# Running sums of the log decays: formed once in the projections and loaded per chunk, instead of formed per chunk by TensorE

## The chip, the cores and the metric

One core of a Trainium2 chip. The engines are TensorE (PE; its weight loads are listed apart as PEld), VectorE (DVE), ScalarE (ACT), GpSimd (POOL) and SyncE (SP), which issues all the DMAs of this kernel. The metric is the device time of one execution in microseconds; the kernel before takes 2838.83 us, the median of three runs (2835.25 to 2843.82).

## The reference

A trunk layer with three token mixers, sequence 2048, width 1024, all float32. The change touches only the third mixer, the gated delta rule (8 value heads, 4 query/key heads of 128), where each head has a scalar log decay per token:

```python
g = jnp.cumsum(log_a, axis=-1)
diff = g[..., :, None] - g[..., None, :]
decay_strict = masked_exp(diff, strict)
decay_causal = masked_exp(diff, causal)
m = jnp.einsum('bhntk,bhnsk->bhnts', k, kb) * decay_strict
sol = lax.linalg.triangular_solve(eye + m, rhs, ...)
a_qk = jnp.einsum('bhntk,bhnsk->bhnts', q, kb) * decay_causal
q_inter = q * jnp.exp(g)[..., None]
k_state = kb * jnp.exp(g_last[..., None] - g)[..., None]
```

So per chunk and head the kernel needs a 128x128 matrix exp(g_t - g_s) for t >= s, the vectors exp(g_t) and exp(g_last - g_s), and exp(g_last).

## The kernel before

Four stages follow one another with barriers between: `norm_and_transpose` (to 84 us), `project` (to 1638), `recur` (to 2287) and `merge`.

`project` forms all projections as 80 pairs of column tiles `p`, with a Strassen-like scheme; ACT rounds each weight block (`high_part`), POOL forms the rest (`low_part`), PE multiplies. At its end POOL fills masks (`fill_masks`), among them `causal`. The log decays of all 16 chunks and 8 heads already lie in SBUF as `ab[:, :, 0:V]`, a token per partition.

`recur` walks 16 chunks (windows) `w` of 128 tokens. The order on each engine is written out by hand, and while window `w` is computed, the preparation of `v = w+1` is woven in. For the decays, POOL multiplies the causal mask by the log decays in two fp32r parts (`log_decays`, L1454, result `la_t`); PE sums them with a mask of later tokens (`decays_between`, L1554 with `later_r`) and with ones (`decays_from_start`, L1554 with `ones_r`), four instructions of 512 columns each; ACT takes the exponentials from PSUM into `dec` and `eg` (L1833, L1839); POOL multiplies `dec` by minus beta (`weighted_decays`, L1464), and DVE makes `ak` and `aq` with it (`an_keys` L2019, `an_queries` L2024).

The inverse of the triangular matrix runs through DRAM. SP writes `ak` out (L1383), waits, and loads its 16x16 diagonal blocks as `X` (L1386). DVE sets their diagonal (`unit_diagonal`, L2028) and substitutes in 14 steps (L2040, L2043), interleaved with its other work; ACT copies the results as `XI` and `XT` (L1904, L1905); SP writes them (L1395, L1397), and loads whole matrices `T` and `R` (L1400, L1403) for window `v`. PE then doubles the block size three times (`level_w`, `level_z`: L1657, L1677 and others). On SP's queue a window is thus: T, R, `zin` (1 MB) and `hin` (1.25 MB) for the window after, the keys (512 KB, `load_k`, landing in `w_raw`), two stores `yh` and `yc` (256 and 512 KB), `ak` out (512 KB), X, and then XI and XT again. `load_k` waits for `keys` of DVE, the stores for the results, `ak` out for DVE's `an_keys`.

Two more waits matter. PE's `products_ds(w, 0)` (the second L1714 of a window) waits for XT of `v`. DVE's first instruction of a window, `pair_kq` (L2058), waits for `hx_inv`, which ACT makes (L1847) after `key_norms`, which waits for PE's `norms` (L1550).

Of the kernel before, what the change touches and what calls it, by code (L numbers as in the profile page):

```python
# [22 lines left out]
P = 128  # L23
# [481 lines left out]
def project(nc, dm, io, keep, front, h_dram, s_dram, y_dram, g_dram):  # L505
# [78 lines left out]
    with ExitStack() as c:  # L584
# [13 lines left out]
        X, Y, Z = ([bank(f"p_{n}{i}") for i in range(2)] for n in "xyz")  # L598
        own_sems = []
# [16 lines left out]
        zeroed, step, masks_set, masks_cut = sem("zeroed"), sem("step"), sem("masks_set"), sem("masks_cut")  # L616

# [14 lines left out]
        t2 = craw[:, 0, :, 3:3 + 2 * BLK]  # L632
        form_place = {P1: wide(work[:]), P5: wide(work[:]), P2: wide(lows_of(P5)), P6: t2, P4: wide(ring[:]), P3: wide(lows_of(P3))}
# [42 lines left out]
        with nc.Block() as block:  # L676
            @block.sync
            def _(sp):
# [37 lines left out]
                for p in range(N):  # L716
                    q = before(p)
# [35 lines left out]
                sp.wait_ge(keys_in, 16)  # L753
                for r in range(RING):
# [4 lines left out]
            def _(pool):  # L759
# [16 lines left out]
                for p in range(N):  # L776
                    for of, j in ((p + 1, P1), (p, P4), (p + 1, P2), (p, P3), (p + 1, P6), (p + 1, P5), (p + 1, P7)):
# [6 lines left out]
                fill_masks(pool, {**keep["masks"], **front["masks"]}, masks_set, masks_cut)  # L784

            @block.tensor
            def _(pe):
# [22 lines left out]

                for p in range(N):
                    q = before(p)
# [22 lines left out]
            def _(act):  # L835
# [108 lines left out]
                for p in range(N):  # L944
                    q, more = before(p), p + 1 < N
# [61 lines left out]
            def _(dve):  # L1007
# [8 lines left out]
                def token_sum(sb, j):  # L1016
# [7 lines left out]
                    elif of == P7:  # L1024
                        if k.start == 0:
                            dve.wait_ge(b_in["b22"], 16 * sb)
                        else:
# [193 lines left out]
                for p in range(N):  # L1221
                    q, more = before(p), p + 1 < N
# [52 lines left out]
def recur(nc, dm, io, keep, front, lead, s_dram, y_dram):  # L1275
# [18 lines left out]
    with ExitStack() as c:  # L1294
# [3 lines left out]
        col, neg_b = sb("col", [P, 3, win, V]), sb("neg_b", [P, win, V])  # L1298
        la_parts = sb("la_parts", [P, 2, win, V], F32R)
        la_t = sb("la_t", [P, 2, V, P], F32R)  # L1300
        ones_r, later_r = sb("ones_r", [P, P], F32R), sb("later_r", [P, P], F32R)
# [25 lines left out]
        count(m_ssq=2, m_ga=2, m_gb=2, m_kq=2, m_vt=2, m_ks=2, m_kt=1, m_hvt=1, m_w=2 * levels, m_z=2 * levels,  # L1327
              m_hs=7, m_e=2, m_o=2, m_ds=2, m_hkt=1, m_ho=1, m_hds=1, m_hn=1, m_n=2)
        count(rn_ready=4, dec_ready=2, eg_ready=2, vt_ready=2, kt_ready=1, hv_ready=1, w_ready=2 * levels,
# [1283 lines left out]
```

## Time and profile before

| | |
|---|---|
| median of 3 runs | 2838.83 us (2835.25 to 2843.82) |
| span of the profiled execution, first to last instruction | 2836.0 us |
| own time of that execution beyond its span | not listed; the median is 2.8 us above the span |
| PE busy, PEld busy | 2729.1 us (96%), 2284.9 us (81%) |
| DVE, ACT, POOL busy | 1843.0, 1240.6, 1471.9 us |
| DMA | 366.05 MB, 45.0% of 16 engines |

The page gives averages over four stages, and the change acts on one of them, so the stage `recur` is read by itself: its engines' busy time by window, the timeline of one window, and the order of SP's issues. A number in brackets behind a timeline row is how long the engine stood idle before it, and what released it. TensorE's clock is 1.00 of full in the steady windows; it is at half in part of window 0.

### The profile page before, as it was taken

How to read it: one execution, taken by the hardware profiler on the slowest of the kernel's cores; microseconds unless marked ns; L12 is line 12 of the kernel's file. 1: busy time of each engine (PE TensorE's matmuls, PEld its weight loads, DVE VectorE, ACT ScalarE, POOL GpSimd, SP SyncE). 2: the span in 40 equal slices, each digit the busy share in tenths (PEclk: the TensorE clock that was granted, in tenths of full speed). 3: DMA queues.
4: the chain of work that ended last, by engine and by line, in shares of the span. 5: the costliest groups of instructions: out<-in, count | busy, mean ns of one | idle time of the engine just before them, and what ended most of it. 6: DMA issues, size and time to landing. Idle time of an engine off the chain costs nothing. (4 is left out here: it accounts for less than half of the span.)

```text
span 2836.0 us, 39388 instructions
## 1 busy us (share of the span) xinstructions
PE 2729.1 (96%) x14135; PEld 2284.9 (81%) x14135; DVE 1843.0 (65%) x2902; ACT 1240.6 (44%) x2154; POOL 1471.9 (52%) x1135
## 2 busy tenths in 40 slices
PE   6899999999998999999999979999999989999999
PEld 5788888888886888888888868888888867888887
DVE  6677777773338788888732258888888855445453
ACT  6443444444444434343444335565556533222221
POOL 0545555454445455555544556667776534453541
PEclk9999999999999999999999979999999989999999
DMA  5333333333453333333334356555556557455552
GB/s 173 99 110 97 112 91 103 108 107 91 119 158 115 122 97 106 88 112 108 97 101 119 97 145 154 146 134 132 134 152 155 135 173 239 157 183 169 177 174 76
DMA packets 536937, 366.05 MB, mean 129 GB/s; under 512 B 65462, under 2 KB 469032, under 8 KB 536744
## 3 DMA queue, kind: packets, MB, share of 16 engines
q1 hardware_dynamic: 536744, 363.52, 45.0%
q8 instruction: 115, 1.88, 0.3%
q14 instruction: 78, 0.64, 0.1%
HBM read 251.27 MB, written 112.20 MB: 128 GB/s over the span
## 5 line engine op out<-in xcount | busy, mean ns | idle before, releaser
L767 POOL TENSOR_TENSOR w_low<-w_raw,w_high 128x512 fp32r<-128x512 f32 x480 | 686.1, 1435 | 635.7 <-ACT w_high L845 635.7
L799 PE MATMUL p_x<-h_high,w_high 128*128 128x512 f32 x1280 | 501.1, 391 | 16.8 <-POOL w_low L767 7.5
L799 PE MATMUL p_x<-h_low,w_high 128*128 128x512 f32 x1280 | 500.5, 391 | 0.0
L799 PE MATMUL p_x<-h_high,w_low 128*128 128x512 f32 x1280 | 500.5, 391 | 0.0
L845 ACT ACTIVATE w_high<-w_raw 128x512 fp32r<-128x512 f32 x480 | 297.1, 626 | 246.3 <-PE p_z L799 139.9
L799 PEld LDWEIGHTS p_x<-h_high,w_high 128*128 128x128 f32 x1280 | 241.7, 189 | 69.3 <-POOL w_low L767 7.6
L799 PEld LDWEIGHTS p_x<-h_low,w_high 128*128 128x128 f32 x1280 | 241.7, 189 | 50.5
L799 PEld LDWEIGHTS p_x<-h_high,w_low 128*128 128x128 f32 x1280 | 241.7, 189 | 50.2
L799 PE MATMUL p_z<-h_high,w_low 128*128 128x512 f32 x640 | 249.0, 389 | 0.0
L799 PE MATMUL p_z<-h_high,w_high 128*128 128x512 f32 x640 | 249.0, 389 | 0.0
L799 PE MATMUL p_z<-h_low,w_high 128*128 128x512 f32 x640 | 249.0, 389 | 0.0
L2407 PE MATMUL b_o<-m_yh,m_wo_high 128*128 128x512 f32 x512 | 201.2, 393 | 19.1 <-DVE m_yl_lead L2543 12.5
L1090 DVE TENSOR_TENSOR c_raw<-p_z,u 128x512 f32<-128x512 f32 x72 | 49.8, 691 | 245.2 <-PE p_x L799 188.9
L2368 POOL TENSOR_TENSOR m_wo_low<-m_wo_raw_lead,m_wo_high 128x512 fp32r<-128x512 f32 x86 | 117.8, 1372 | 172.6 <-ACT m_wo_high L2462 172.6
L2407 PE MATMUL b_o<-m_yh,m_wo_low 128*128 128x512 f32 x512 | 200.4, 391 | 0.0
L767 POOL TENSOR_TENSOR w_low<-w_s,w_high 128x512 fp32r<-128x512 f32 x80 | 114.9, 1436 | 98.0 <-ACT w_high L845 97.3
L1106 DVE SCALAR_TENSOR_TENSOR ring<-c_raw,cols,ring 128x512 f32<-128x512 f32 x128 | 142.3, 1112 | 4.6
L1475 POOL TENSOR_TENSOR dx<-hin 128x256 f32<-128x256 f32 x112 | 76.6, 684 | 130.7 <-ACT hx L1858 117.5
L2506 DVE TENSOR_TENSOR w_raw<-b_o,ring 128x512 f32<-128x512 f32 x96 | 65.9, 691 | 118.2 <-PE b_o L2407 97.0
L799 PEld LDWEIGHTS p_z<-h_high,w_high 128*128 128x128 f32 x640 | 120.1, 188 | 25.1 <-DVE c_raw L1090 0.2
L799 PEld LDWEIGHTS p_z<-h_low,w_high 128*128 128x128 f32 x640 | 120.1, 188 | 24.9
L799 PEld LDWEIGHTS p_z<-h_high,w_low 128*128 128x128 f32 x640 | 120.1, 188 | 24.9
(299 smaller groups left out, 6082.2 us busy)
## 6 DMA issues: line engine op xcount, KB each, us to landing
w_raw<-in_w_in_dram SPq DMA_DIRECT2D x160, 512.0 KB, 5.2
branch_scratch<-ring SPq DMA_DIRECT2D x176, 256.0 KB, 5.2
gate_scratch<-ring SPq DMA_DIRECT2D x96, 256.0 KB, 6.0
ring<-gate_scratch SPq DMA_DIRECT2D x96, 256.0 KB, 4.0
hin<-branch_scratch SPq DMA_DIRECT2D x16, 1280.0 KB, 11.4
zin<-branch_scratch SPq DMA_DIRECT2D x16, 1024.0 KB, 7.0
m_wo_raw_lead<-in_w_out_c_dram SPq DMA_DIRECT2D x43, 256.0 KB, 3.0
xin<-in_x_dram SPq DMA_DIRECT2D x16, 512.0 KB, 4.0
```

The lines of the kernel that those rows point to most:

```text
L767: nc.gpsimd.tensor_tensor(wl[:, j, :, :], place(p, j), wh[:, j, :, :].bitcast(F32), ALU.subtract).then_inc(low, 1)
L799: x = nc.tensor.matmul(to[:], w[:, j, k, :], h[:, j, k, :], start=(opens and k == 0 and a == 0), stop=(k == HK - 1 and a == 2), skip_group ...
L845: fn(wh[:, j, :, :], place(p, j), ACT.Copy).then_inc(high, 1)
L1090: tt(of_unit(p, 1, 1), Z[p % 2][:], u3[:], ALU.add).then_inc(c22, 1)
L1106: link(stt(out, src, w, out, ALU.mult, ALU.add))
L1475: tt(free_ap(dx[:, l % 2, :], 0, halves), left, mid, ALU.subtract)
L2368: tt(wl[:, u % SLOTS, :, :], wraw(u), raw(wh[:, u % SLOTS, :, :]), ALU.subtract).then_inc(w_low, 1)
L2407: x = nc.tensor.matmul(bank, w[:, u % SLOTS, k, :], y(4 * i + k), start=(i < 3 and k == 0 and a == 0), stop=(i != 2 and k == 3 and a == 2))
L2506: tt(to, bank, gt[:, b, :], ALU.mult).then_inc(gated, 1)
```

## The change

In `project`, PE forms once four sums over all chunks (causal, after, all, and `centred`, the sum counted from the middle of the chunk) into PSUM before pair 8; ACT copies them at pair 9; PE transposes two of them before pair 10, ACT copies at 11, and SP writes both to DRAM at pair 12. `causal` is filled by POOL before pair 3, two masks by DVE at pair 6. In `recur`, SP loads per chunk two rows of 1024 sums spread over all 128 partitions (512 KB each, 4 KB per partition): `rows_centred` and `rows_start`. POOL subtracts the column sums and takes the minimum with 0 (`exponents`); ACT takes the exponentials from SBUF. The eight matrix instructions of L1554 of each chunk, `log_decays`, and `columns` are gone, and the waits on PSUM banks that they needed.

```diff
@@ project, PE
+                    for i, which in enumerate((causal[:], after, keep["ones"][:], centred)):
+                        x = nc.tensor.matmul(sums_bank[:, i, :], which, ab[:, :, 0:dm.vh], start=True, stop=True)
+                    for i, at in enumerate((0, 3)):
+                        x = nc.tensor.transpose(rows_bank[:, i, :], kept_sums[:, at, :], keep["ident"][:])
@@ recur, SP
+                def load_centred(v):
+                    wait(sp, v - 1, "diff_ready", 1)
+                    sp.dma_start(rows_centred[:].rearrange("p h n -> p (h n)"), bass.AP(rows.tensor, (win + v) * V * P, [[0, P], [1, V * P]])
+                                 ).then_inc(centred_in, 16)
+                def load_start(v):
+                    wait(sp, v - 1, "eg_ready", 1)
+                    sp.dma_start(rows_start[:].rearrange("p h n -> p (h n)"), bass.AP(rows.tensor, v * V * P, [[0, P], [1, V * P]])
+                                 ).then_inc(start_in, 16)
...
+                sp.dma_start(col[:].rearrange("p i w c -> p (i w c)"), front["decay_sums"]).then_inc(col_in, 16)
+                load_centred(0)
+                load_start(0)
                 load(0)
...
                         blocks_out(w + 1)
+                        if w + 2 < win:
+                            load_start(w + 2)
                         inverses_back(w + 1)
+                        if w + 3 < win:
+                            load_centred(w + 3)
@@ recur, POOL
-                def log_decays(v):
-                    wait(pool, v - 1, "m_ga", 2)
-                    for i in range(2):
-                        tt(la_t[:, i, :, :], free_ap(masks["causal"][:], 0, [[0, V], [1, P]]), spread(la_parts[:, i, v, :].bitcast(F32), P),
-                           ALU.mult).then_inc(sems["la_ready"], 1)
+                def exponents(v):
+                    pool.wait_ge(centred_in, 16 * v + 16)
+                    wait(pool, v - 1, "aq_ready", 2)
+                    tt(dec[:], rows_centred[:], spread(col[:, 3, v, :], P), ALU.subtract).then_inc(sems["diff_ready"], 1)
+                    wait(pool, v, "diff_ready", 1)
+                    nc.gpsimd.tensor_scalar(dec[:], dec[:], 0.0, None, ALU.min).then_inc(sems["diff_ready"], 1)
@@ recur, PE (main loop)
-                    if 0 < w < win - 1:
-                        decays_between(v)
                     level_z(w, 4)
...
-                    if 0 < w < win - 1:
-                        decays_from_start(v)
                     level_w(w, 5)
@@ recur, ACT
+                    wait(act, v, "diff_ready", 2)
                     for g in range(2):
-                        wait(act, v, "m_gb", g + 1)
-                        fn(four(dec, g), M[g][:], ACT.Exp).then_inc(sems["dec_ready"], 1)
+                        fn(four(dec, g), four(dec, g), ACT.Exp).then_inc(sems["dec_ready"], 1)
...
-                    for g in range(2):
-                        wait(act, v, "m_ga", g + 1)
-                        fn(four(eg, g), M[2 + g][:], ACT.Exp).then_inc(sems["eg_ready"], 1)
+                    act.wait_ge(start_in, 16 * v + 16)
+                    fn(eg[:], rows_start[:], ACT.Exp).then_inc(sems["eg_ready"], 1)
```

PE's row in a steady window, before (b_m are PSUM banks, `la_t` the masked log decays):

```order
6879 L1657 MATMUL b_g<-T,ak 128x64 x8
6880 L1604 MATMUL b_m<-ident,qkn 128x128 x4
6881 L1610 MATMUL b_m<-ident,hin 128x128 x4
6882 L1554 MATMUL b_m<-la_t,later_r 128x512 x4
6883 L1677 MATMUL b_g<-W,R 128x64 x8
6884 L1577 MATMUL b_m<-qkn 128x256 x4
6885 L1628 MATMUL b_h<-kql 128x128 x4
6886 L1554 MATMUL b_m<-la_t,ones_r 128x512 x4
6887 L1657 MATMUL b_g<-T,ak 128x64 x8
```

and the same place after:

```order
6875 L1697 MATMUL b_g<-T,ak 128x64 x8
6876 L1644 MATMUL b_m<-ident,qkn 128x128 x4
6877 L1650 MATMUL b_m<-ident,hin 128x128 x4
6878 L1717 MATMUL b_g<-W,R 128x64 x8
6879 L1619 MATMUL b_m<-qkn 128x256 x4
6880 L1668 MATMUL b_h<-kql 128x128 x4
6881 L1697 MATMUL b_g<-T,ak 128x64 x8
```

Eight instructions between the first and the second `level_w` are gone, and nothing else moved.

SP's queue in a steady window, after (`w_raw` is where the keys land):

```order
200 L1453 DMA T<-inverse_scratch 128x8x128
201 L1456 DMA R<-inverse_scratch 128x8x128
202 L1407 DMA rows_centred<-decay_rows_scratch 128x1024
203 L1424 DMA zin<-branch_scratch 128x16x128
204 L1425 DMA hin<-branch_scratch 128x20x128
205 L1418 DMA w_raw<-branch_scratch 128x8x128
206 L1430 DMA y_scratch<-yh 128x4x128
207 L1432 DMA y_scratch<-ring 128x8x128
208 L1436 DMA an_scratch<-ak 128x8x128
209 L1439 DMA X<-an_scratch 64x16x16
210 L1412 DMA rows_start<-decay_rows_scratch 128x1024
211 L1448 DMA inverse_scratch<-XI 64x16x16
```

The row is that of before, with `rows_centred` put in ahead of `zin` and `rows_start` put in behind X.

SP's queue at the start of `recur`, after; before, the five rows of `col`, `rows_centred` and `rows_start` are not there:

```order
176 L1468 DMA col<-decay_sums_scratch 128x512
177 L1407 DMA rows_centred<-decay_rows_scratch 128x1024
178 L1412 DMA rows_start<-decay_rows_scratch 128x1024
179 L1424 DMA zin<-branch_scratch 128x16x128
180 L1425 DMA hin<-branch_scratch 128x20x128
181 L1474 DMA inverse_scratch<-S 128x8x128 x2
182 L1418 DMA w_raw<-branch_scratch 128x8x128
183 L1407 DMA rows_centred<-decay_rows_scratch 128x1024
184 L1412 DMA rows_start<-decay_rows_scratch 128x1024
185 L1436 DMA an_scratch<-ak 128x8x128
186 L1439 DMA X<-an_scratch 64x16x16
```

All five added loads of the start stand ahead of the first `ak` out and the first X.

## Rows read from the trace of the kernel before

**Rows 1.** Busy us by stretch: PE, PEld, DVE, ACT, POOL, clock, DMA share, GB/s.
```profile
1757.76:1795.45 37.69, 37.06 (x296) 32.89 (x295) 31.88 (x91) 22.56 (x44) 26.70 (x24) 1.00 0.58 146
1720.07:2212.85 492.78, 483.11 (x3824) 427.99 (x3823) 414.74 (x1170) 292.98 (x560) 347.17 (x312) 1.00 0.58 145
```
**Rows 2.** Timeline of PE, one window: start us, duration us, line, output and inputs.
```profile
1761.11 1.22 PE L1554 MATMUL b_m<-la_t,later_r 128*128 128x512 f32 x4
1762.17 1.89 PE L1677 MATMUL b_g<-W,R 128*128 128x64 f32 x16
...
1765.68 1.05 PE L1628 MATMUL b_h<-kql 128*128 128x128 f32 x8
1766.49 1.17 PE L1554 MATMUL b_m<-la_t,ones_r 128*128 128x512 f32 x4
1767.49 1.90 PE L1657 MATMUL b_g<-T,ak 128*128 128x64 f32 x16
...
1785.80 1.06 PE L1714 MATMUL b_m<-e,ks 128*128 128x128 f32 x8
...
1791.09 1.88 PE L1550 MATMUL b_m<-w_raw,ones 128*128 128x512 f32 x4
```
**Rows 3.** Timeline of DVE, the same window: its ends and its waits.
```profile
1757.76 0.69 DVE L2058 TENSOR_TENSOR kql<-hin,hx_inv 128x512 f32<-128x512 f32 x1 [2.30 <-ACT hx_inv L1847]
...
1774.55 0.07 DVE L2028 MEMSET X<- 64x16 f32 x1
...
1782.76 0.42 DVE L2079 COPY A<-b_h 64x256 f32<-64x256 f32 x1 [0.21 <-PE b_h L1630]
...
1795.45 0.69 DVE L2058 TENSOR_TENSOR kql<-hin,hx_inv 128x512 f32<-128x512 f32 x1 [2.24 <-ACT hx_inv L1847]
```
**Rows 4.** Timeline of ACT, end of the same window.
```profile
1784.82 0.38 ACT L1904 ACTIVATE XI<-b_m 64x256 f32<-64x256 f32 x1 [2.15 <-DVE b_m L2043]
1785.10 0.36 ACT L1905 ACTIVATE XT<-b_m 64x256 f32<-64x256 f32 x1
```
**Rows 5.** Timeline of SP's DMA issues: start us, us of issuing.
```profile
1750.79 0.37 SPq L1400 DMA_DIRECT2D T<-inverse_scratch  x1
...
1762.77 0.36 SPq L1365 DMA_DIRECT2D w_raw<-branch_scratch  x1
...
1766.89 0.36 SPq L1383 DMA_DIRECT2D an_scratch<-ak  x1
1770.77 0.60 SPq L1386 DMA_DIRECT2D X<-an_scratch  x1
...
1788.46 0.37 SPq L1400 DMA_DIRECT2D T<-inverse_scratch  x1
```
**Rows 6.** DMA issues in 1740 to 2200 us: KB each, median us to landing.
```profile
X<-an_scratch SPq DMA_DIRECT2D x12, 64.0 KB, 2.7
```
**Rows 7.** Waits in 1740 to 2200 us: us in total, times, longest.
```profile
DVE X L2028 <- DMA X<-an_scratch: 2.2, 4, 0.9
```
**Rows 8.** DMA in 1750 to 1776 us, 40 slices of 0.65 us.
```profile
DMA  3004899999999999999998699999997100550000
GB/s 49 0 9 97 243 345 329 292 289 291 289 291 291 289 294 299 291 290 290 290 290 214 169 291 354 333 345 349 344 346 235 39 0 0 50 51 0 0 0 0
```
**Rows 9.** Timeline of POOL, the same window.
```profile
1763.17 2.37 POOL L1464 TENSOR_TENSOR dec<-dec,db 128x1024 f32<-128x1024 f32 x1 [3.11 <-ACT dec L1833]
1765.49 1.90 POOL L1489 TENSOR_TENSOR ks<-kt,col 128x1024 f32<-128x1024 f32 x1
...
1770.32 3.75 POOL L1454 TENSOR_TENSOR la_t<-causal,la_parts 128x1024 fp32r<-128x1024 f32 x2
```
**Rows 10.** Start of `recur`: DMA in 1640 to 1656 us, 40 slices of 0.4 us.
```profile
GB/s 159 128 236 324 337 348 346 302 287 274 283 297 298 298 293 287 289 289 291 294 310 344 348 346 344 348 348 346 346 348 347 343 343 346 338 195 37 0 0 0
```
**Rows 11.** Start of `recur`, SP: the first X issued.
```profile
1655.12 0.68 SPq L1386 DMA_DIRECT2D X<-an_scratch  x1
```
**Rows 12.** Start of `recur`, PE: the first `level_w` of window 0.
```profile
1679.18 3.62 PE L1657 MATMUL b_g<-T,ak 128*128 128x64 f32 x16
```

More of the change, by code:

```diff
@@ L598, in project @@
         X, Y, Z = ([bank(f"p_{n}{i}") for i in range(2)] for n in "xyz")
+        sums_bank, rows_bank = (c.enter_context(nc.psum_tensor(f"p_sums{i}", [P, 4, P], F32)) for i in range(2))
+        causal = keep["masks"]["causal"]
+        ab = keep["ab"][:, 0:dm.win * 2 * dm.vh].rearrange("p (w c) -> p w c", c=2 * dm.vh)
         own_sems = []
@@ L1221, in _ @@
                 for p in range(N):
+                    if p == 6:
+                        dve.wait_ge(causal_cut, 1)
+                        tt(centred, causal[:], spread(causal[:, P // 2 - 1:P // 2], P), ALU.subtract).then_inc(sum_masks, 1)
+                        tt(after, keep["ones"][:], causal[:], ALU.subtract).then_inc(sum_masks, 1)
                     q, more = before(p), p + 1 < N
@@ L1297, in recur @@
         hin, zin, kin = sb("hin", [P, 2, NH, P]), sb("zin", [P, 2, NZ, P]), front["keys"]
[L1298 to L1301, printed above, removed]
+        col, neg_b = sb("col", [P, 4, win, V]), sb("neg_b", [P, win, V])
+        rows_centred, rows_start = sb("rows_centred", [P, V, P]), sb("rows_start", [P, V, P])
         db, dec, eg = sb("db", [P, V, P]), sb("dec", [P, V, P]), sb("eg", [P, V, P])
@@ L1507, in _ @@
                 differences(0, 1)
-                log_decays(1)
+                exponents(1)
                 betas(1)
@@ L1536, in _ @@
                 mm, turn, ident = nc.tensor.matmul, nc.tensor.transpose, keep["ident"][:]
-                def columns():
-                    for i, which in enumerate((masks["causal"][:], later_r[:].bitcast(F32), keep["ones"][:])):
-                        x = mm(G[0][:, i, :], which, ab[:, :, 0:V], start=True, stop=True)
-                    x.then_inc(m_col, 1)
                 def norms(v):
@@ L1550, in norms @@
                         mm(M[g][:], keep["ones"][:], sq[:, g, :], start=True, stop=True).then_inc(sems["m_ssq"], 1)
-                def sum_parts(bank, which, g):
-                    for i in range(2):
-                        x = mm(bank[:], which[:], four(la_t[:, i, :, :], g), start=(i == 0), stop=(i == 1))
-                    return x
-                def decays_between(v):
-                    wait(pe, v, "la_ready", 2)
-                    wait(pe, v, "rn_ready", 3)
-                    for g in range(2):
-                        wait(pe, v - 1, "res", 4 * g + 4)
-                        sum_parts(M[g], later_r, g).then_inc(sems["m_gb"], 1)
-                def decays_from_start(v):
-                    if v > 0:
-                        wait(pe, v - 1, "hv_ready", 1)
-                        wait(pe, v - 1, "kt_ready", 1)
-                    for g in range(2):
-                        sum_parts(M[2 + g], ones_r, g).then_inc(sems["m_ga"], 1)
                 def products_kq(v):
@@ L1850, in level_exp @@
                     elif l == 2:
-                        wait(act, w + 1, "eg_ready", 2) if more else wait(act, w, "kt_ready", 1)
+                        wait(act, w, "kt_ready", 1)
                     elif l == 3:
@@ L1854, in level_exp @@
                     elif l == 4:
-                        wait(act, w + 1, "eg_ready", 1) if more else wait(act, w, "hv_ready", 1)
+                        wait(act, w, "hv_ready", 1)
                     else:
```

100 lines of the change are left out of this document (59 added, 41 removed).

## The prediction

> **What bounds the kernel now.** First the busy time by stretch, taken for one quiet window and for 13 windows [rows 1]. It shows the window's period, 37.69 us in the quiet one and 492.78/13 = 37.91 on average, and PE busy for 98% of it. That number invites the reading that PE sets the pace, so the second view is the timeline of one window, engine by engine, asking which instruction starts just when its releaser ends.
>
> PE's rows [rows 2] stand almost without gaps, but that only says that matmuls overlap. DVE's rows [rows 3] are the ones to follow: from 1757.76 to the end of the substitution just before 1784.82, 27 us, DVE waits once, 0.21 us. ACT's XI then starts after an idle time of 2.15 us, straight on the last step of DVE [rows 4]. XT ends at 1785.46, and PE's second L1714, which waits for it, starts at 1785.80 [rows 2, 4]: 0.3 us of slack. From there PE runs on without a hole to `norms` at 1791.09, ACT makes `rn` and then `hx_inv` from that, and DVE, idle for 2.24 us until `hx_inv` is there, starts the next window at 1795.45 [rows 2 to 4]. So a circle closes in 37.69 us: 27.1 us of DVE, 10.6 us of ACT, PE, ACT. Call it circle A. All eight removed matmuls lie outside it, while DVE is busy.
>
> The second circle is the DMA queue's. T issued at 1750.79, X issued at 1770.77, DVE's `unit_diagonal` at 1774.55, XI at 1784.82, T again at 1788.46 [rows 3 to 5]. X lands 2.75 us after its issue (its median by the DMA view is 2.7) [rows 6], so at 1773.5: 1.05 us before DVE wants it. Without that slack circle B takes 20.0 (T to X) + 2.75 + 10.27 (diagonal to XI) + 3.64 (XI to T) = 36.66 us. It has almost no reserve: in 4 of 12 windows DVE waited for X [rows 7], and these make the mean 37.91 instead of 37.69. From T to X the 16 engines are nearly saturated: 285 to 345 GB/s without a break but for a dip at 1763.6 to 1764.6 [rows 8].
>
> **The matmuls removed in the windows.** L1554 costs PE 1762.17 - 1761.11 = 1.06 and 1767.49 - 1766.49 = 1.00 us, start to start [rows 2]: 2.06 us per window, 14 windows, 29 us if PE set the pace. But DVE doesn't wait for PE in circle A except for the 0.21 us [rows 3], which goes, and the 0.3 us before the second L1714, of which I count 0.2, since a semaphore's passing stays. Circle A falls to 37.3 us. The rest of the 2 us becomes idle time of PE before that L1714 and before L1655. Bounds: 0 and 0.5 us per window.
>
> What the Trainium skill says here comes by itself. Its page "Perfetto Trace Analysis", section "Identifying the Most-Contended Engine", names matmul busy time a poor measure, LDWEIGHTS busy a good one, and says to optimize the engine that comes out highest first. By that rule it is PE here (32.89 of 37.69 us, 87%, against DVE's 85%), and the change would earn its 2.06 us per window. The timeline speaks against it, by the 27 us in which DVE hardly waits; the rule's outcome is the first rival.
>
> **POOL.** `log_decays` took 3.75 us [rows 9]. The subtraction is a 128x1024 operation with one spread operand, like L1489, 1.90 us. The minimum isn't in the trace; with one tensor read in place of two I take 1.5, between 0.9 (half of L1489) and 2.3 (a full two-input product, L1464, 2.37). Together 3.4, between 2.8 and 4.2, in the place of 3.75, and two microseconds before anything waits: nothing either way.
>
> The Trainium skill's "GPSIMD Engine Reference", section "Engine selection", puts one-input operations at about line rate; with its 1.03 cycles per element at 1.2 GHz that is an estimate of 0.9 us. No row here shows such an operation, and the sum would be the same by it.
>
> **ACT.** The exponentials have the same width; `eg` no longer waits for PE, but nobody on a circle waits for it. Nothing.
>
> **The loads in the windows.** `rows_start` (512 KB) goes out behind X, when the queue is empty for about 12 us [rows 8]: free. `rows_centred` (512 KB, 0.52 MB) goes out behind R and ahead of `zin`, into the saturated stretch of circle B. At 345 GB/s it takes 1.5 us, at 290 1.8; bounds 1.3 and 1.9. How much reaches X? Bytes flow 2.0 us after an issue (T at 1750.79, bytes from 1752.75). T, R, zin, hin fill the queue to 1764.0, with the new load to 1765.5. The keys are issued at 1762.77 by DVE's leave, so their bytes couldn't start before 1764.8; now they start at 1765.5. Keys and two stores, 1.31 MB at 345, end at 1769.3. `ak`, issued at 1766.89, could flow from 1768.9 in any case; now from 1769.3. So X slips by some 0.3 to 0.4 us of the 1.5, because two dips swallow the rest. Bounds: 0 and the whole 1.8. I take 0.3: circle B becomes 36.66 + 0.3 - 0.2 (the DVE wait for PE at L2079 lies in it too) = 36.8 us, still under circle A's 37.3 in quiet windows. Nine quiet windows win 0.4 each, 3.6 us; the four or so in which the queue runs late lose 0.1 each. Sum for the windows 1 to 13: -3.2 us. The last prepared window has no `rows_centred` in its queue: -0.4.
>
> **The start of `recur`.** Here the queue is saturated at about 290 to 348 GB/s from 1641 to 1654 [rows 10], and X is issued right when it empties, at 1655.12 [rows 11]; DVE's substitution waits for it. The change puts 0.26 + 4 x 0.52 = 2.36 MB ahead of it: 6.8 us at 345. X then comes 6.8 us later. In return, between the substitution and `level_w` at 1679.18 [rows 12] PE no longer waits through two groups of sums and ACT through their exponentials: about 2 to 2.5 us. I take +4.5 us, bounds +2 and +8. PE runs at half speed there (3.62 us for the sixteen instructions that take 1.90 later [rows 2, 12]); I leave that as it is, though another pattern of idle time ahead may shift it by some 6 us either way.
>
> **In `project`** PE is the pace, and four products of 128 columns are 0.2 us each (0.81 us from the first L1628 group of four heads to the next row [rows 2]), two transposes no more than that: +1.1 us, bounds 0.5 and 3. ACT's two copies, DVE's two small masks and POOL's mask fall into idle times of one to three microseconds at these places. If POOL's doesn't, PE waits once, 0.6 us. SP's wait at pair 12 is for a copy one pair old.
>
> **Sum.** 2836.0 + 1.1 + 4.5 - 3.2 - 0.4 = 2838.0 us of span, 2.0 more than before. The median stands 2.8 us above the span: 2841 us, against 2838.8.
>
> **Rivals.**
> 1. *PE sets the pace.* For it, 98% busy and 87% of weight loads [rows 1]; against it, circle A. The time: 2836 + 5.6 - 29 + 2.8 = 2815 us. 4%.
> 2. *The clock at the start.* PE reaches full speed sooner in window 0, or the start costs its lower bound of 2 us, and the windows give their 0.5: 2836 + 1 + 2 - 6 - 6 + 2.8 = 2830 us. 10%.
> 3. *Slower: the queue.* The dips don't swallow the load, and all of its 1.5 to 1.8 us reaches X. Then circle B is 36.66 - 0.2 + 1.5 = 38.0 us in the quiet windows (+0.3) and 1.3 more in the late ones: 9 x 0.3 + 4 x 1.3 = +8 us, and with 5.6 for start and project 2836 + 13.6 + 2.8 = 2852; with 1.8 us 2856. It decides from the point where more than about 0.9 us of the load reaches X. For it: DVE waits for X already in a third of the windows [rows 7]. Against it: the dips [rows 8]. 25%.
> 4. *Slower: the start*, by its upper bound of 8 us and a longer half speed: 2850 us. 7%.
> 5. *The loads aren't spread at full rate*, since all 128 partitions read the same 4 KB. At half rate 3 us would stand in the queue of each window: 2870. 2%.
>
> **How the numbers follow.** A change under 0.3% (8.5 us) can't be told from none. The forecast, with its own range 2835 to 2847, gets 52%. Faster by over 0.3%, under 2830.3: rival 1, most of rival 2: 12%. Slower, over 2847.3: rivals 3 to 5, mostly: 32%. Within: 56%. The range leaves out rival 1, rival 5 and the upper end of rival 3: 2830 to 2855.
>
> **What would show it.** Eight PE rows fewer per window, and idle time of PE before L1655 and the second L1714. The period, DVE's `kql<-hin,hx_inv` start to start: 37.3 in quiet windows if I am right, 38 if rival 3, 35.6 if rival 1. T to X issue: 20.3 against 20.0, or 21.5. More waits of DVE for X. The first X at 1663 instead of 1655, both counted with project's microsecond. A granted clock of 1.00 in window 0 would be rival 2. The forecast is wrong if the period moves by more than 0.5 us or the start by more than 8.

## The result, and the profile after

| | before | after |
|---|---|---|
| median of 4 runs each, us | 2840.91 | 2886.39 (2880.75 to 2889.78) |
| ratio | 1 | 1.0173, interval 1.0153 to 1.0192 |
| span of the profiled execution, us | 2836.0 | 2883.4 |
| its mean granted clock of TensorE | 0.984 | 0.967 |
| windows 1 to 13, us | 492.8 | 530.5 |
| of these, windows with a granted clock of 1.00 | 13 | 2 |

The change makes the kernel 1.7% slower; the forecast was no change. Divided at DVE's `kql<-hin,hx_inv`, which opens each window, the 47.4 us of span fall like this: up to window 1 +3.4 (1720.07 to 1723.42), windows 1 to 13 +37.7, the last prepared window +4.3 (35.35 to 39.69), the rest +2.0.

The busy time by stretch, as in [rows 1] (PE, PEld, DVE, ACT, POOL, granted clock, DMA share, GB/s): one window, the 13 windows, one of the two windows at full clock, the last prepared window, and 4 us inside the first of these.

```profile
1763.78:1804.23 40.45, 37.42 (x288) 33.23 (x287) 31.82 (x90) 22.25 (x43) 27.64 (x24) 0.96 0.60 164
1723.42:2253.89 530.47, 495.10 (x3720) 441.08 (x3719) 411.20 (x1170) 289.10 (x547) 359.36 (x312) 0.94 0.61 160
1968.23:2006.83 38.60, 35.80 (x288) 31.62 (x287) 31.51 (x91) 22.29 (x43) 27.59 (x24) 1.00 0.62 157
2253.89:2293.58 39.69, 36.42 (x270) 33.64 (x269) 32.06 (x91) 19.94 (x39) 19.71 (x21) 0.87 0.44 108
1785.00:1789.00 4.00, 4.00 (x24) 4.00 (x23) 2.39 (x9) 1.19 (x2) 4.00 (x4) 0.57 0.00 0
```

Eight matmuls fewer in the window (288 against 296), and yet PE is busy longer, 37.42 against 37.06 us. The last row says why: for some microseconds of the window the granted clock is at its lower level, 1.2 instead of 2.4 GHz. At full clock PE is busy for 35.80 us, 1.26 less than before; the prediction had put the removed products at 2.06, start to start.

PE in the same window (start us, duration us, idle time before and its releaser):

```profile
1778.01 0.68 PE L1695 MATMUL b_g<-T,ak 128*64 128x64 f32 x8 [0.65 <-DVE T L2127]
1779.32 0.68 PE L1695 MATMUL b_g<-T,ak 128*64 128x64 f32 x8 [0.63 <-DVE T L2127]
...
1782.65 1.10 PE L1674 MATMUL b_h<-kql 128*128 128x64 f32 x8 [0.44 <-DVE kql L2096]
1784.46 3.33 PE L1725 MATMUL b_g<-w_raw,R 128*128 128x128 f32 x16 [0.71 <-DVE R L2132]
```

Four short waits for DVE (two more, of 0.36 and 0.21 us, stand just ahead of them), and then the sixteen products of L1725 take 3.33 us. The window of before has one such wait, and the same sixteen products take 2.00 us:

```profile
1773.59 0.68 PE L1655 MATMUL b_g<-T,ak 128*64 128x64 f32 x8 [0.59 <-DVE T L2104]
...
1777.36 2.00 PE L1685 MATMUL b_g<-w_raw,R 128*128 128x128 f32 x16
```

In this window the fall of the clock comes after a stretch of small products with short waits, not after one long rest. The 9 us that end about there, in busy time by stretch, first before, then after:

```profile
1770.00:1779.00 9.00, 8.37 (x90) 7.75 (x90) 8.42 (x29) 4.44 (x9) 9.00 (x9) 1.00 0.09 12
```

```profile
1776.00:1785.00 9.00, 6.33 (x61) 5.52 (x61) 7.03 (x24) 3.71 (x8) 8.91 (x9) 1.00 0.39 114
```

PE was busy for 8.37 of these 9 us and is now for 6.33. It has run through its row faster, since the sums are gone from it, and DVE, which was late for X, holds it up.

SP's issues, the answer to [rows 5]:

```profile
1797.26 0.36 SPq L1453 DMA_DIRECT2D T<-inverse_scratch  x1
1797.72 0.53 SPq L1456 DMA_DIRECT2D R<-inverse_scratch  x1
1798.30 1.34 SPq L1407 DMA_DIRECT2D rows_centred<-decay_rows_scratch  x1
1799.80 0.36 SPq L1424 DMA_DIRECT2D zin<-branch_scratch  x1
1800.21 5.02 SPq L1425 DMA_DIRECT2D hin<-branch_scratch  x1
1809.24 0.41 SPq L1418 DMA_DIRECT2D w_raw<-branch_scratch  x1
...
1813.19 1.28 SPq L1436 DMA_DIRECT2D an_scratch<-ak  x1
1818.92 0.60 SPq L1439 DMA_DIRECT2D X<-an_scratch  x1
1819.57 0.65 SPq L1412 DMA_DIRECT2D rows_start<-decay_rows_scratch  x1
```

T to X is 21.66 us here (21.67 on the mean of 13 windows; 20.64 before, 20.0 in its quiet window). `ak` goes out 15.93 us after T, as before (16.10); all of the delay is behind it: 5.73 us from there to X instead of 3.88, since the queue is that much fuller. X also lands later behind its issue, 3.2 us in the median of 1740 to 2200 us where it was 2.7 [rows 6], with `rows_start` issued right behind it. What DVE waits for, in the stretch of [rows 7] (us in total, times, longest), and DVE in the window:

```profile
DVE X L2051 <- DMA X<-an_scratch: 20.3, 12, 2.9
DVE A L2106 <- PE b_h L1674: 20.0, 13, 2.4
```

```profile
1781.87 0.07 DVE L2051 MEMSET X<- 64x16 f32 x1 [1.54 <-DMA X<-an_scratch]
```

Before, the first was 2.2 us in 4 windows [rows 7] and the second 0.4 us, once. DVE now waits for X in every window, and once more for PE while PE is at half speed. POOL's pair, with mean ns:

```profile
L1522 POOL TENSOR_SCALAR dec<-dec 128x1024 f32<-128x1024 f32 x13 | 36.0, 2766 | 1.1
L1520 POOL TENSOR_TENSOR dec<-rows_centred,col 128x1024 f32<-128x1024 f32 x13 | 24.7, 1897 | 0.0
```

The minimum takes 2.77 us, so the pair takes 4.66 in the place of 3.75. And the first X of `recur`, the answer to [rows 11]:

```profile
1662.64 0.67 SPq L1439 DMA_DIRECT2D X<-an_scratch  x1
```

### The profile page after: what moved, and what is told of

It reads as the page before. It is cut to its first block and busy times, and to the rows that moved or that the text cites. A ratio compares the mean times of both kernels' runs of the same rounds, so it can differ in the third digit from the quotient of the medians.

```text
span 2883.4 us, 39177 instructions
## 1 busy us (share of the span) xinstructions
PE 2745.6 (95%) x14011; PEld 2301.1 (80%) x14011; DVE 1832.6 (64%) x2900; ACT 1236.3 (43%) x2140; POOL 1490.3 (52%) x1135
## 3 DMA queue, kind: packets, MB, share of 16 engines
q8 instruction: 114, 1.87, 0.3%
## 5 line engine op out<-in xcount | busy, mean ns | idle before, releaser
L814 PE MATMUL p_x<-h_high,w_low 128*128 128x512 f32 x1280 | 500.5, 391 | 0.0
```

The costliest lines, as they stand in the source:

```text
L814: x = nc.tensor.matmul(to[:], w[:, j, k, :], h[:, j, k, :], start=(opens and k == 0 and a == 0), stop=(k == HK - 1 and a == 2), skip_group ...
```

## Experiments

"13 windows" is the time from window 1 to window 14 in the profiled execution, "low" the number of those windows with a granted clock under 1.00, "full" the mean of the others. Ratios are to the kernel before on the same chip in the same session.

| kernel | ratio, interval | 13 windows | low | full | T to X | first X |
|---|---|---|---|---|---|---|
| before | 1 | 492.8 | 0 | 37.91 | 20.6 | 1655.1 |
| after | 1.0173 (1.0153 to 1.0192) | 530.5 | 11 | 38.45 | 21.7 | 1662.6 |
| e1 | 1.0094 (1.0073 to 1.0115) | 518.0 | 9 | 37.41 | 20.4 | 1662.0 |
| e2 | 1.0071 (1.0056 to 1.0085) | 512.8 | 4 | 38.47 | 21.8 | 1654.7 |
| e3 | 1.0092 (1.0074 to 1.0109) | 500.9 | 4 | 37.45 | 20.4 | 1663.1 |
| e4 | 1.0123 (1.0103 to 1.0143) | 526.6 | 8 | 38.75 | 22.0 | 1661.6 |
| f1 | 1.0038 (1.0014 to 1.0061) | 500.9 | 3 | 37.82 | 20.6 | 1661.8 |
| f2 | 1.0025 (1.0007 to 1.0042) | 498.1 | 3 | 37.56 | 20.6 | 1655.3 |
| f4 | 1.0049 (1.0031 to 1.0068) | 490.6 | 0 | 37.74 | 20.5 | 1664.4 |
| f5 | 1.0041 (1.0027 to 1.0055) | 500.5 | 3 | 37.64 | 20.6 | 1662.5 |
| g1 | 1.0085 (1.0061 to 1.0109) | 505.2 | 4 | 37.86 | 20.5 | 1659.4 |
| g2 | 1.0005 (0.9984 to 1.0026) | 496.6 | 1 | 37.94 | 20.6 | 1655.0 |
| g5 | 1.0066 (1.0043 to 1.0088) | 495.2 | 2 | 37.66 | 20.6 | 1657.5 |
| h1 | 1.0060 (1.0037 to 1.0083) | 496.6 | 2 | 37.83 | 20.6 | 1660.7 |
| h2 | 1.0047 (1.0029 to 1.0065) | 498.9 | 1 | 38.18 | 20.5 | 1661.3 |
| h3 | 1.0144 (1.0122 to 1.0167) | 528.6 | 8 | 39.72 | 20.4 | 1662.0 |

The number of low windows changes from one execution to the next, so a single profile tells it only roughly; the ratios carry the verdicts, the profile says where the time lies.

**e1, `rows_centred` loaded behind X.**

```diff
                             load_start(w + 2)
+                        if w + 3 < win:
+                            load_centred(w + 3)
                         inverses_back(w + 1)
-                        if w + 3 < win:
-                            load_centred(w + 3)
```

> The changed kernel with one edit: in the window loop rows_centred is issued behind rows_start, after X and ahead of XI, when the queue is empty, instead of ahead of zin. Theory Q (the queue): rows_centred delays ak out and X, and that alone makes the circle T, X, substitution, XI longer. Then T to X issue falls back from 21.7 to 20.0-20.4 us, DVE stops waiting for X, PE's half-speed stretches in the windows go, the period falls from 40.8 to 37.3-37.8 us, and the time to some 2840-2848 us. Rival P (POOL): the minimum takes 2.76 us, the POOL pair 4.66 instead of 3.75, and everything behind it on POOL is late; then the period stays above 39.5. Rival C (clock): without the eight matmuls PE idles and falls to half speed whatever the queue does; then T to X falls but the stretch from unit_diagonal to XI stays near 11.7 us and the period near 39.

Measured: 2859.62 against 2835.0 us, about half of the loss gone. T to X is back at 20.4 us. The windows now come in two kinds (total, a low one, a full one):

```profile
1726.24:2244.26 518.02, 494.66 (x3720) 441.99 (x3719) 412.10 (x1171) 289.46 (x547) 358.98 (x312) 0.93 0.62 163
1763.36:1803.99 40.63, 38.73 (x288) 34.70 (x287) 31.81 (x91) 22.32 (x43) 27.62 (x24) 0.92 0.61 161
1726.24:1763.36 37.12, 35.52 (x288) 31.59 (x287) 31.49 (x90) 22.22 (x43) 27.58 (x24) 1.00 0.69 176
```

The full ones last 37.12 to 38.01 us, 37.41 on the mean; the prediction had 37.3 for circle A. The same work at 0.92 costs 3.2 us more of PE time and 3.5 us more of window. DVE's waits for X are down from 20.3 us to 4.5 in 5 windows (before: 2.2 in 4), and 9 windows are still slow: the place of the load is one cause of two. Theory Q had T to X right and the clock wrong; the full windows speak against rival P, and the low ones are as rival C said.

**e2, the kernel before with two 512 KB loads at the new places.** The loads fetch other data spread over partitions, into a buffer that is free then.

```diff
                         blocks_out(w + 1)
+                        if w + 2 < win:
+                            load_extra(1, w)
                         inverses_back(w + 1)
+                        if w + 3 < win:
+                            load_extra(0, w)
```

> The kernel before, unchanged in its arithmetic, with two loads of 512 KB spread over partitions (4 KB read by all) added in the window loop at the places of rows_centred and rows_start, into a buffer that nothing reads. Theory Q: the loads alone bring the loss: T to X issue 21.5 us, X later by 0.5 us behind its issue, period 38.5-40.5 instead of 37.9, time 2850-2880. If the loss needs the missing matmuls as well (rival C), the clock stays 1.00 in the windows, unit_diagonal to XI stays 10.3, and the period is 38.5: time about 2850. Rival P expects no change at all: 2841.

Measured: 2852.23 against 2835.0 us. T to X 21.8, a full window 38.47, which is what after's full windows take; and four windows low, though all sums are there, which rival C had excluded. The time, 2852, is the one that both theories had as possible.

**e3, the changed kernel without the loads.** The rows of windows 0 and 1 are loaded, later windows reuse them and so have the decays of another chunk.

```diff
                 def load_centred(v):
+                    if v > 1:
+                        return
...
-                    pool.wait_ge(centred_in, 16 * v + 16)
+                    pool.wait_ge(centred_in, 16 * min(v, 1) + 16)
```

> The changed kernel without the loads of rows for the chunks 2 to 15: all use the rows of chunk 1, so the decays are those of a wrong chunk; every instruction of POOL, ACT, DVE and PE stays. Theory Q: circle B is as before, period 37.3-37.6, time about 2840. Rival P: period above 39.5, as in the changed kernel. Rival C: the clock falls below 1.00 in the windows and the period is 38.5-39.5.

Measured: 2860.09 against 2835.0 us, like e1. Without any row traffic the full windows take 37.45 as in e1 (37.41): behind X the loads cost the period nothing, though X itself lands in 2.7 us here and in 3.2 in e1. What is left is the clock, as rival C said, 4 windows in this profile, and the start.

**e4, the changed kernel with eight unused matmuls per window**, 128x512, at the two places where the sums had stood.

```diff
+                def filler(bank):
+                    for _ in range(2):
+                        mm(bank[:], fill_a, fill_b, start=True, stop=True)
...
+                    if 0 < w < win - 1:
+                        fill_between(v)
                     level_z(w, 4)
...
+                    if 0 < w < win - 1:
+                        fill_start(v)
                     level_w(w, 5)
```

> The changed kernel with eight matmuls of 512 columns per window (ones by ones, result unused) put back at the two places of the removed ones; loads as in the changed kernel. Rival C: they keep PE at full speed, unit_diagonal to XI falls from 11.7 to 10.3 us and the period from 40.8 to 39.3: time about 2867. Theory Q with the queue as the only cause: X comes as late as in the changed kernel, T to X 21.7; the matmuls lie in PE's idle time, so the time stays 2880-2890 if the half speed comes from the waiting for X itself.

Measured: 2869.54 against 2835.0 us, a ratio of 1.0123 for 1.0173, so 0.5% is back; 8 windows still low. Rival C's time, 2867, came out, but not its full speed; T to X is 22.0, so X is as late as in the changed kernel.

**f1, both edits, of e3 and of e4: no loads, eight unused matmuls.**

> The changed kernel with the row loads only for windows 0 and 1 (later windows reuse their rows, so the decays are those of the wrong chunk) and with eight 128x512 matmuls per window that nothing reads, at the two places where the removed sums stood. Theory (two independent losses: the extra loads lengthen T to X by 1.5 us, and TensorE with less work falls to half clock in part of the windows, about 3 us each): with both taken back the granted clock is 1.00 in every window, the period 37.3 to 37.8 us, and the time is within 6 us of the kernel before (2835 to 2843 on its chip's 2838). Rival (the slower pair on POOL, 4.66 against 3.75 us, or the later start of the recurrence carries much of it): the period stays at 38.5 us or more with the clock at 1.00, time 2850 or more.

Measured: 2843.29 against 2837.49 us, 5.8 more: inside the theory's 6, against the rival's 2850. Not as expected is that three windows in a row fell to 0.92 in the profiled execution (one of the longer ones, 2856.92 us); the ten full ones take 37.82, mostly 37.69.

**f2, the kernel before without its sums.** From window 2 on, four 128x8 products stand for the eight of 128x512, and the exponentials are of zero (decays of 1). No loads are added.

```diff
-                def sum_parts(bank, which, g):
+                def sum_parts(bank, which, g, v):
+                    if v >= 2:
+                        return mm(bank[:, 0, 0:8], which[:], la_t[:, 0, 4 * g, 0:8], start=True, stop=True)
...
-                        fn(four(dec, g), M[g][:], ACT.Exp).then_inc(sems["dec_ready"], 1)
+                        fn(four(dec, g), M[g][:], ACT.Exp, scale=0.0 if v >= 2 else 1.0).then_inc(sems["dec_ready"], 1)
```

> The kernel before in which, from window 2 on, the eight 128x512 sum matmuls of a window are four of 128x8 (with the exponential of zero in their place, so decays of 1); no loads are added. Theory (less TensorE work alone lets the clock fall): TensorE's granted clock falls to 0.92 to 0.96 in a third to two thirds of the windows, the period there is 40 to 41.5 us, and the time is 12 to 25 us above the kernel before. Rival (the clock falls only because of the added loads): clock 1.00 in every window, period 37.3 to 37.7 us, time 0 to 6 us below the kernel before.

```profile
1945.19:1982.31 37.12, 35.84 (x292) 31.98 (x291) 31.42 (x90) 22.36 (x44) 26.65 (x24) 1.00 0.59 148
2056.93:2098.57 41.64, 39.50 (x293) 35.50 (x292) 31.53 (x91) 22.24 (x44) 26.74 (x24) 0.92 0.59 147
```

Measured: 2843.04 against 2837.49 us. The rival fell, since the clock does fall without any added load, in 3 of 13 windows; the theory had its sign right and its size two to four times too large (5.5 us instead of 12 to 25). Taking these matmuls out of each window, with the exponentials' input as the only other edit, makes this kernel slightly slower: 0.35 us gained on the mean of the windows that keep their clock (0.6 in the quiet ones, 37.11 for 37.69), 2.6 to 4.1 us lost in one that doesn't. The kernel before isn't free of such falls either, although its profile shows none: on this chip its 35 runs took 2823.9 to 2848.5 us at mean clocks from 0.989 down to 0.981.

**f4, `rows_centred` behind X, and eight unused matmuls** (e1 and e4 together).

> The changed kernel with the load of rows_centred issued right behind that of rows_start (behind X), and with eight 128x512 matmuls per window that nothing reads at the two places where the removed sums stood. Theory (loads before X cost 1.5 us a window, missing TensorE work costs the clock): T to X 20.2 us, clock 1.00 in at least 11 of 13 windows, period 37.5 us, time within 8 us of the kernel before. Rival (a filler at the old places does not keep the clock, as in the run with filler alone, where the clock still fell in 7 windows): half the windows at 0.92 with a period of 40 to 41.5 us, time 2855 to 2862.

```profile
1766.23:1803.92 37.69, 37.06 (x296) 32.89 (x295) 31.68 (x91) 22.19 (x43) 27.59 (x24) 1.00 0.66 173
1728.54:2219.18 490.64, 482.18 (x3824) 427.80 (x3823) 409.34 (x1170) 288.72 (x547) 358.76 (x312) 1.00 0.66 172
```

Measured: 2848.07 against 2837.49 us. In the profile no window is low, and the 13 take 490.6 us, 2.1 less than before: nothing of the 37.7 us is left, with POOL's longer pair in place. Its span is 2844.2, 8.2 over before's, and 8.5 more are there already when window 1 starts (1728.54 against 1720.07). So in this execution these two causes are all of what the windows lost, and the start is a third. Of the 8.5 us, 4.5 are there when window 0 starts (1656.35 against 1651.83); the other 4.0 lie in window 0, which ran at a clock of 0.66 against 0.70. Other executions of it ran to 2866.65 us at a lower mean clock (0.973), so filler makes the falls rarer (by the ratios of e1 and f4, 1.0094 and 1.0049) and doesn't end them.

**f5, four unused matmuls where PE waits** (e1, and two ahead of each group of `level_w` at level 6; none at the old places).

```diff
                     for g in range(2):
+                        if l == LEVELS - 1 and 0 < w < win - 1:
+                            wait(pe, w, "h_pred", 2)
+                            filler(HB[1])
```

> The changed kernel with the load of rows_centred behind that of rows_start, and with only four 128x512 matmuls per window that nothing reads, two ahead of each of the two groups of level_w at level 6, where TensorE waits 0.65 and 0.63 us for VectorE right before the clock falls. Theory (it is the half idle stretch around the level steps that brings the clock down): clock 1.00 in nearly all windows, period 37.2 to 37.5 us, time within 6 us of the kernel before or below it. Rival (what counts is the work of the whole window, so four matmuls of eight give half): clock 0.92 in a third of the windows, time 2845 to 2852.

Measured: 2850.06 against 2837.49 us; three low windows in the profile. By ratio it can't be told from f4, with half the filler; the rival's number came out (2845 to 2852).

**g2, the kernel before with both extra loads behind X.**

```diff
                             load_extra(1, w)
-                        inverses_back(w + 1)
                         if w + 3 < win:
                             load_extra(0, w)
+                        inverses_back(w + 1)
```

> The kernel before with the same two added 512 KB loads a window as in the earlier run, but both issued right behind the load of X, where the queues are idle. Theory (only where the loads stand costs time: behind XI's write they share the queues with zin, hin and the keys and set X back by 1.5 us): T to X 20.2 us instead of 21.7, period 37.7 us, clock 1.00, time within 3 us of the kernel before. Rival (the traffic itself costs, wherever it stands): T to X 21 us or more, or diagonal and X 1 us later, time 8 to 17 us above.

```profile
1716.79:2213.34 496.55, 486.27 (x3824) 431.24 (x3823) 414.69 (x1171) 292.96 (x560) 347.26 (x312) 0.99 0.65 170
```

Measured: 2840.13 against 2837.02 us, a ratio of 1.0005. The same 1 MB per window that cost 17 us in e2 costs nothing that can be told from zero when all of it is issued between X and XI: T to X 20.6, full windows 37.94 as before, one low window. It is the place, not the traffic.

**g1, f4 with the rows of window 1 behind the first X.**

```diff
                 load_centred(0)
-                load_start(0)
                 load(0)
+                load_start(0)
...
-                load_centred(1)
-                load_start(1)
                 blocks_out(0)
                 load(1)
+                load_centred(1)
+                load_start(1)
```

> The changed kernel with rows_centred loaded behind X, eight unused 128x512 matmuls per window at the old places, and at the start of the recurrence the rows of window 1 loaded behind the first X instead of ahead of the first keys' write (and those of rows_start of window 0 behind zin and hin). Theory (of the 8 us that the same kernel without the last edit still lost in its profile, most is the first X, issued at 1664.4 against 1655.1 us, because 1 MB of rows stands ahead of it): the first X is issued at 1658 to 1660, the first two windows start 4 to 6 us earlier, the time is 2840 to 2845, within 0.3% of the kernel before. Rival (the start is held by the subtraction and minimum on POOL and by the code behind it, not by the queue): first X at 1662 or later, time unchanged at 2848.

Measured: 2860.09 against 2837.02 us, worse than f4. The first X does come at 1659.43, as the theory had it, but window 1 starts at 1737.07, 8.5 us later than in f4: POOL's `exponents(1)` now waits for its row behind `hin`, and the second substitution with it. Neither theory had the time: the rival expected 2848 and a late X. It was right only in that this edit gains nothing.

**h1, f4 with only the second `load_start` moved back.**

> The changed kernel with rows_centred behind X and eight unused matmuls a window, where at the start of the recurrence only the second load of rows_start is moved behind the first X and behind zin and hin; the second load of rows_centred stays ahead of the keys' write. Theory (at the start both places of a row load cost: ahead of the keys' write it delays the first X, behind it the second window's decays; only rows_start is free to go back): first X issued at 1661 to 1663 against 1664.4, window 2 starts 2 to 4 us before 1740.0, time 2842 to 2848, at least not above the 2848.1 of the same kernel without this edit. Rival (the start cannot be had back by order alone): window 2 at 1740 or later, time 2848 to 2855.

Measured: 2848.49 against 2836.48 us. X at 1660.7, window 1 at 1724.98, 3.6 us before f4's, as expected, but over all runs no better than f4 (ratio 1.0060 against 1.0049, times from 2845.5 to 2863.2): what the start gives is less than the scatter of the runs.

**g5, f5 with six unused matmuls and g1's start.**

> As the run with rows_centred behind X and gap filler, with three instead of two unused 128x512 matmuls ahead of each group of level_w at level 6 (six a window), and with the later rows at the start. Theory (more TensorE work in the window, no matter where, means fewer falls of its clock): at most one or two windows below a clock of 1.00, period 37.2 to 37.7 us elsewhere, first X at 1658 to 1660, time 2838 to 2845. Rival (the falls do not depend on this work): three or more windows at 0.92 to 0.96 and a time of 2846 or more.

Measured: 2855.21 against 2837.02 us. Two low windows, the rest 37.66, as the theory had it; window 1 starts at 1734.64, so the start alone costs 14.6. The time is the rival's, but for the reason found in g1.

**h2, f4 with twelve unused matmuls.**

> The changed kernel with rows_centred behind X and twelve unused matmuls a window: eight at the old places and four ahead of level_w at level 6. Theory (the more TensorE has to do in a window, the rarer its clock falls, at the price of the work itself): no window below 1.00 in the profile, all timed runs within 8 us of each other, period 37.8 to 38.6 us, time 2848 to 2858. Rival (the clock falls by something else than TensorE's own work, such as the other engines or the DMA): again two or more windows at 0.92 and a spread of 15 us or more.

Measured: 2849.69 against 2836.48 us; one low window, though PE is busy for 497.69 of 498.86 us; the six times lie within 9.4 us of each other, f4's twelve within 21.7. Twelve instead of eight cost 0.4 us per window and gain nothing by the ratio (1.0047 against 1.0049); the narrower scatter fits the theory, which had 8 us, but six runs on another chip don't show it. The one low window is also the one in which DVE waited longest for X, and PE behind it, at a place where its quiet windows have no wait at all:

```profile
1930.79 0.07 DVE L2077 MEMSET X<- 64x16 f32 x1 [1.47 <-DMA X<-an_scratch]
```

```profile
1933.39 3.64 PE L1745 MATMUL b_g<-w_raw,R 128*128 128x128 f32 x16 [0.71 <-DVE R L2158]
```

**h3, f4 with the minimum done twice.**

```diff
+                    if v > 1:
+                        nc.gpsimd.tensor_scalar(dec[:], dec[:], 0.0, None, ALU.min).then_inc(sems["min_ready"], 1)
+                        wait(pool, v - 2, "min_ready", 1)
```

> The changed kernel with rows_centred behind X and eight unused matmuls a window, with the minimum on POOL done twice from window 2 on (the result is the same), so that POOL has 2.76 us more in a window. Theory (POOL's work is hidden in the steady windows, so the minimum's 2.76 us, above what had been taken for it, costs nothing there): period 37.7 us, time 2845 to 2852, as without the second minimum. Rival (POOL's pair is on the way to the keys' decays): period 38.5 us or more, time 2858 or more.

Measured: 2876.66 against 2836.48 us; by the ratios (1.0144, 1.0049) some 27 us more than f4. I had POOL hidden, and the rival was right. ACT in one full window of h3 (39.73 us long), and at the same place of f4:

```profile
1948.13 0.60 ACT L1907 ACTIVATE b_m<-dx 128x512 f32<-128x512 f32 x1 [3.54 <-POOL dx L1548]
```

```profile
1784.46 0.60 ACT L1904 ACTIVATE b_m<-dx 128x512 f32<-128x512 f32 x1 [0.95 <-POOL dx L1545]
```

POOL's five `dx` behind the pair come 2.8 us later, ACT's exponential of them 2.6 us later (3.54 against 0.95 of waiting), and DVE, which waits for nothing there in f4, waits 1.87 us. A full window takes 39.72 instead of 37.74: of 2.77 us more on POOL 2.0 reach the period. POOL's slack behind the pair is 0.8 us, not the two microseconds that I had read. And 8 of the 13 windows are low, though eight matmuls are there and DVE waits at most 0.72 us for X in any of them: here DVE is late because of POOL.

## Why the prediction was wrong

Forecast 2841 us, range 2830 to 2855, measured 2886.4. Step by step:

- **The matmuls and circle A.** Right: 37.3 us predicted for a quiet window at full clock, 37.11 measured in e1, e3 and f2 (37.4 to 37.6 on the mean of their full windows); the gain of 0.6 us is just over the upper bound of 0.5. Rival 1 (PE sets the pace, 35.6 us) never showed. The rule of the Trainium skill weighed there ("Perfetto Trace Analysis", "Identifying the Most-Contended Engine") would have had this change earn 2 us per window; f2 earned at most 0.6 where the clock held.
- **"How much reaches X".** Wrong, and one of the two steps on which the forecast failed. I let two dips in the queue swallow 1.2 of the 1.5 us. The dip ahead of the keys was no reserve: with and without the load `w_raw` and `ak` are issued at the same distance from T (11.98 and 15.9 us in after and e1), and the difference stands whole between `ak` and X, 5.73 against 4.21 us. Circle B is 38.45, not 36.8. Rival 3 had the mechanism and nearly the size (38.0 in quiet windows; after's two full ones take 38.31 and 38.60); by e1 against after it is 1.04 us per window, 13.5 us. g2 shows that the place decides. `rows_start`, called free, has a part in it: with it right behind X, X lands in 3.2 us instead of 2.7 (after and e1; 2.7 again in e3). The rates of [rows 8] run from 289 to 354 GB/s outside the dip, those of [rows 10] between 1641 and 1654 go down to 274, not 285 and 290 as I wrote; that changes no term.
- **The clock in the windows.** Missing. I wrote of the clock at the start only and took 1.00 for granted in the windows because the trace of before has it there [rows 1]. In the sum of after's 13 windows it is the largest term: 530.5 - 13 x 38.45 = 30.6 us, in 11 windows (38.45 rests on only two full windows, but e2's nine give 38.47). The other terms are 13 x (38.45 - 37.41) = 13.5 for the loads and 13 x (37.41 - 37.91) = -6.5 for the removed work; together 37.6 of 37.7. The last prepared window, predicted -0.4, lost 4.3, with its clock down too (0.87, against 1.00 in f4, whose window takes 35.36).
- **POOL.** The minimum was priced at 1.5 us, bounds 0.9 and 2.3; it takes 2.77, outside both. It cost nothing in the windows only because 0.8 us of slack remained (h3); two microseconds "before anything waits" was wrong. The estimate of 0.9 us from the Trainium skill ("GPSIMD Engine Reference", "Engine selection") is off by a factor of 3 for this operation, and my upper bound, taken from the two-input rows, was too low as well.
- **The start and `project`.** +5.6 predicted, +3.4 in after, 8.5 in f4, inside the bounds of 2.5 to 11. First X at 1662.6 for 1663 predicted. The clock of window 0, left as it is in the forecast, scatters by more than the loads cost: the window takes 68.2 us at 0.70 (before and after), 72.2 at 0.66 (f4), 57.3 at 0.88 (e2).
- **Rivals' chances.** A third of the weight lay on slower, none of it beyond 2870. Rival 3 as it stands gives 2852 to 2856. What was missing was not a mishap but a mechanism: work that is off every circle can still help to hold the clock up.

What makes the clock fall is shown only in part. By low windows in the profiled executions:

| | rows behind X, or none | a load ahead of zin and hin |
|---|---|---|
| no sums, no filler | e1, e3, f2: 16 of 39 | after: 11 of 13 |
| eight big matmuls | before, f1, f4, g1, g2, h1: 10 of 78 | e2, e4: 12 of 26 |

Not in the table are the runs with other amounts of filler, rows behind X (f5 with four 3 of 13, g5 with six 2, h2 with twelve 1), and h3 with eight and the second minimum: 8 of 13.

Both the missing work and DVE's being late (which leaves PE with short waits) raise the count, and together they make it nearly every window. The counts are of one execution each; the ratios agree (e4 below after, f4 below e1, g2 below e2). Window by window, outside h3: of the 21 windows in which DVE waited 1.5 us or more for X, all 21 are low; of the 34 with a wait of 1.0 to 1.5 us, 13; of the 140 with less or none, 21 (the limits were set with the counts in view). h3 shows that it need not be X that DVE waits for.

After lost 45 us, where e2 (17) and f2 (5.5) and the start (about 8) add up to 30. That the two causes strengthen each other is one reading. But e3, without any late load, already lost 25 us, where f2 and the start add up to 14. f2 kept four small products and the shorter pair on POOL (3.75 for 4.66 us), and no run separates these, so a part of POOL in the falls is neither shown nor excluded.

The Trainium skill's page "TensorE: Matmul & The Clock Gate", section "A second HAM failure mode: psum-queue depth-cycling", has TensorE's clock swing where it idles briefly and often. The trace agrees so far: the longest idle time of PE in the row before the fall at 1785 is 0.71 us. But in a low window of f1 PE has a single wait of 0.60 us at that place, in a full window of f4 one of 0.59, with DVE waiting 0.30 us for X in the one and not at all in the other; the next two windows of f1 fell too, with no wait for X, and none of f4 did in its profile. Why one window falls and its twin doesn't stays open.

No version ran faster than the kernel before. The best of the changed ones, f4 and f5, lose 0.4 to 0.5%, most of it at the start of `recur`; g1 and h1 show that the order of the queue there doesn't give it back.

## What to carry to other kernels

Before taking work from TensorE, price its clock too: a window in which it fell to half its level for a while cost 1.5 to 3.7 us on the mean of a run (2.8 in after), and one that kept it gained 0.6 at most from the removed matmuls. Put an added load where the queue is idle by the timeline (behind X it cost the period nothing, ahead of `zin` 0.5 us per full window by e2 and g2, 1.0 by after and e1), and don't let a dip in the throughput count as room unless the next issue behind it really moves. And look at who waits for an engine (ACT waited 0.95 us for POOL in f4) before calling it hidden at 73% busy.

## What the runs showed that I had not expected

- POOL's TENSOR_SCALAR minimum, one input, 128x1024 fp32, takes 2.77 us; the two-input subtraction of the same shape with one spread operand takes 1.90, a full two-input product 2.38.
- Eight matmuls fewer per window made PE's busy time longer (495.1 against 483.1 us in 13 windows), since the rest ran at a mean granted clock of 0.94.
- One 512 KB load per window, issued ahead of XI instead of ahead of `zin`, is worth 0.7% of the kernel (e2 at 1.0071, g2 at 1.0005), with the same bytes.
- A wait of DVE for X of 1.5 us or more came with a fallen clock in all 21 windows that had one.
